# Output and down projections: the left half of the columns over all rows first, beside the side work

## What is computed

```python
def reference(x, ...):
    x = first_block(x, ...)     # mixer (delta rule and HGRN heads), FFN, mixer (NSA attention), FFN
    return second_block(x, ...) # mixer (dilated and MoBA), mixer (differential and stick-breaking), norm
# each mixer: h = rmsnorm(x); proj = h @ w_in; y = heads(proj); y @ w_out is added to x (normed in block 1)
# each FFN:   h = rmsnorm(x); silu(h @ w_gate) * (h @ w_up) @ w_down, normed, added to x
```

## Time and profile before

| what | value |
|---|---|
| time, median of 3 runs | 3078.3 us (3074.62 to 3086.6) |
| time of the profiled execution | 3074.2 us |
| its span, first to last instruction | 3072.4 us |
| TensorE busy | 2878.3 us (94%) |
| VectorE, ScalarE, GpSimd busy | 52%, 46%, 7% |
| mean granted TensorE clock | 0.967 |

### The profile page before, as it was taken

How to read it: one execution, slowest core, us unless ns; L and a number is a source line. 1 busy time by engine, 2 the same in 40 slices (tenths; PEclk the granted TensorE clock), 3 DMA queues, 4 the chain that set the end, 5 groups by cost and what they waited for, 6 DMA issues and landing times.

```text
span 3072.4 us, 33268 instructions
## 1 busy us (share of the span) xinstructions
PE 2878.3 (94%) x13558; PEld 2375.6 (77%) x13558; DVE 1609.7 (52%) x2004; ACT 1401.4 (46%) x2037; POOL 225.2 (7%) x209
## 2 busy tenths in 40 slices
PE   7899999899999999999899989999999999979887
PEld 6788787687888888888777767788888888767665
DVE  5664566646455445445334444655445544555545
ACT  6554444545444444334334444644444433454554
POOL 0112223300000000000100100000000000011011
PEclk9999999999999999999889989999999999988888
DMA  6655443655666666555444424566666655634323
GB/s 201 119 119 129 83 98 83 137 188 175 190 187 190 190 189 189 189 191 194 154 136 136 116 65 155 179 187 192 189 188 189 188 191 190 201 113 137 117 90 109
DMA packets 212777, 480.85 MB, mean 157 GB/s; under 512 B 15249, under 2 KB 16273, under 8 KB 211985
## 3 DMA queue, kind: packets, MB, share of 16 engines
q1 hardware_dynamic: 210272, 467.57, 52.3%
q0 software_dynamic: 2352, 11.17, 1.0%
HBM read 476.58 MB, written 2.10 MB: 156 GB/s over the span
## 4 chain that ended last, share of the span: by engine, by line
PE 80%; DVE 7%; ACT 6%; issue 2%; POOL 2%; DMA 2%; SPq 0%; DVEq 0%; ACTq 0%; POOLq 0%
PE PS L962 17%; PE PS L963 16%; PE PS L964 16%; PE PS L1012 7%; PE PS L1013 7%; PE PS L1011 7%; DVE XL L1948 1%; DVE WL L1948 1%; PE PS L1261 1%; ACT BIG L1531 1%; DVE WORK L2091 1%; PE PS L1341 1%; DVE UTL L1984 1%; PE PS L1122 1%; PE PS L1037 1%
## 5 line engine op out<-in xcount | busy, mean ns | idle before, releaser
L1948 DVE TENSOR_TENSOR WL<-RAW,WH 128x1024 fp32r<-128x1024 f32 x819 | 1016.1, 1241 | 995.1 <-ACT WH L1482 994.3
L1482 ACT ACTIVATE WH<-RAW 128x1024 fp32r<-128x1024 f32 x823 | 867.1, 1055 | 954.4 <-PE PS L964 601.6
L962 PE MATMUL PS<-WH,UTH 128*128 128x512 f32 x2396 | 965.2, 403 | 13.4 <-DVE WL L1948 11.9
L963 PE MATMUL PS<-WL,UTH 128*128 128x512 f32 x2396 | 941.6, 393 | 0.0
L964 PE MATMUL PS<-WH,UTL 128*128 128x512 f32 x2396 | 941.4, 393 | 0.0
L962 PEld LDWEIGHTS PS<-WH,UTH 128*128 128x128 f32 x2396 | 455.9, 190 | 111.8 <-DVE WL L1948 14.3
L964 PEld LDWEIGHTS PS<-WH,UTL 128*128 128x128 f32 x2396 | 454.5, 190 | 98.8
L963 PEld LDWEIGHTS PS<-WL,UTH 128*128 128x128 f32 x2396 | 455.6, 190 | 91.2 <-issue 2.5
L1013 PE MATMUL PS<-WH,HTL 128*128 128x512 f32 x656 | 259.3, 395 | 0.0
L1012 PE MATMUL PS<-WL,HTH 128*128 128x512 f32 x656 | 258.8, 394 | 0.0
L1011 PE MATMUL PS<-WH,HTH 128*128 128x512 f32 x656 | 255.4, 389 | 0.0
(11 more groups left out here) (422 smaller groups left out, 2694.9 us busy)
## 6 DMA issues: line engine op xcount, KB each, us to landing
RAW<-in_ffn_w_gu SPq DMA_DIRECT2D x352, 512.0 KB, 4.1
RAW<-in_ffn_w_down SPq DMA_DIRECT2D x176, 512.0 KB, 4.5
RAW<-in_ab_w_in SPq DMA_DIRECT2D x128, 512.0 KB, 4.7
RAW<-in_nsa_w_in SPq DMA_DIRECT2D x80, 512.0 KB, 3.6
RAW<-in_w_in SPq DMA_DIRECT2D x64, 512.0 KB, 4.1
RAW<-in_ab_w_out SPq DMA_DIRECT2D x32, 512.0 KB, 4.5
RAW<-in_nsa_w_out SPq DMA_DIRECT2D x32, 512.0 KB, 4.5
RAW<-in_w_out SPq DMA_DIRECT2D x16, 512.0 KB, 4.6
```

The source lines that it names most:

```text
L962: e.matmul(o, lh, wh[:, j], start=k + j == 0, stop=False)
L963: e.matmul(o, lh, wl[:, j], start=False, stop=False)
L1482: e.activation(wh, raw, ACTF.Copy).then_inc(*a_hi.inc(s))
L1948: e.tensor_tensor(wl, raw, wh.bitcast(F32), ALU.subtract).then_inc(*v_lo.inc(s))
```

## The change

The rows of every stage run in another order: half 0 over all k-tiles (`left`), then half 1 (`right`); only half 1's last slots are the crossing (eight, in stages 4 and 5 four). `left` belongs to the stage's `main`, so the side generators go on beside it. The operand transposes `ot` become side generators of their own (`operand`): each stands in the list as soon as the last column chunk has read the k-tiles that it overwrites (`read`) and its heads are made. The statistics and products of half 0 move from the crossing into `right`, six and three slots ahead of its last early one. Banks: half 0 takes banks 0 to 3, half 1 banks 4 to 7; the ring of banks for side work stays 4 to 7 beside `left`, where it had all eight at the end of a stage. `stat` of the odd n and `tmp_n` of the even n now free the banks, where `new_h` did.

Around it: `cm_w(0)` is put ahead of stage 2's tables and waits for the end of stage 1's rows; `tables_2` drops its wait for stage 4's first chunk; the extra weight places and the scratch JUNK lie elsewhere; some waits follow the new order.

The core of the diff:

```diff
+TAIL = {0: 8, 1: 8, 2: 8, 3: 8, 4: 4, 5: 4}
+LEFT = {st: range(n) for st, n in KTILES.items()}
+LEFT[0] = (*range(8, 12), *range(4), *range(12, 16), *range(4, 8))
+
+
 def row_order(st):
 
-    n = KTILES[st]
-    order = [(k, hf) for k in range(n) for hf in range(2)]
-    if st in (1, 3):
-        order[0:4] = [(0, 0), (1, 0), (0, 1), (1, 1)]
-    order[-TAIL:] = [(k, hf) for hf in range(2) for k in range(n - TAIL // 2, n)]
-    return order
+
+    return [(k, 0) for k in LEFT[st]] + [(k, 1) for k in range(KTILES[st])]
...
         for _ in main:
             for g in sides:
                 next(g, None)
-        put("pool", range(8))
         while sides:
             sides = [g for g in sides if next(g, "end") != "end"]
...
                     put("col", st, c, k, o.next_slot(), (0, 1))
+                    if c == len(WIDTHS[st]) - 1:
+                        o.done.add(("read", st, k))
...
-        def both(name, t, part):
-            for n in (1, 0) if part == 0 else (3, 2):
-                put(name, st, t, n)
-
-        for j in range(TAIL):
+        for j in range(n_tail):
             o.prep(min(s[j] + 3, c[0]))
             row(j, 0)
-            if j == 3:
-                put("stat", st, 0, 0)
-                both("tmp_n", 0, 0)
-        both("tmp_n", 0, 1)
-        put("stat", st, 0, 1)
+            if st >= 4 and j < 2:
+                halves(st, j, 0)
+        halves(st, 0, 1)
         if st == 5:
             put("fin_s", 0)
-            for j in range(TAIL):
+            for j in range(n_tail):
                 row(j, 1)
-                if j == 3:
-                    both("tmp_n", 1, 0)
-                    put("fin_y", 0)
-            both("tmp_n", 1, 1)
+            put("fin_y", 0)
+            halves(st, 1, 1)
             put("fin_s", 1)
...
-        put("pool", (1, 2, 3))
-        for j in range(TAIL):
+        put("pool", (2, 3, 4, 5))
+        for j in range(n_tail):
             row(j, 1)
             if j < 2:
                 put("new_h", st, 0, 2 * j)
                 put("new_h", st, 0, 2 * j + 1)
                 o.prep(c[j + 1])
-            if j > 3:
-                put("uth", st + 1, j - 4, 0)
-            if j == 5:
-                put("stat", st, 1, 0)
-                both("tmp_n", 1, 0)
+            if j > n_tail - 5:
+                put("uth", st + 1, j - n_tail + 4, 0)
             if 3 < j < 7:
                 o.prep(c[j - 1])
-        both("tmp_n", 1, 1)
...
-        put("stat", st, 1, 1)
+        halves(st, 1, 1)
         put("pool", (4, 5, 6, 7))
         o.slot += 8
         for j in range(8):
+            if n_tail == 4 and j < 3:
+                o.prep(c[j + 3])
...
-    def rows(st):
-        for k, hf in row_order(st)[:-TAIL]:
+    def halves(st, t, part):
+
+        if st < 4:
+            put("stat", st, t, part)
+        for n in (2 * part + 1, 2 * part):
+            put("tmp_n", st, t, n)
+        if st < 4 and part:
+            put("root", st, t)
+
+    def left(st):
+        for k in LEFT[st]:
+            if st not in (1, 3):
+                yield from need(("ot", st, k - k % 2))
+            put("row", st, k, 0, o.next_slot(), (0, 1))
+            yield
+
+    def right(st):
+        put("warm", "rows", st)
+        early = row_order(st)[KTILES[st]:-TAIL[st]]
+        for i, (k, hf) in enumerate(early):
             put("row", st, k, hf, o.next_slot(), (0, 1))
-            yield
-
-    def out_proj(st):
-        for k in range(0, KTILES[st], 2):
-            put("ot", st, k)
-        put("warm", "rows", st)
-        drain(rows(st))
-        cross(st)
+            if i in (len(early) - 6, len(early) - 3):
+                halves(st, int(i == len(early) - 3), 0)
+
+    def operand(st, k, *made):
+        yield from need(("read", st, k), *made)
+        put("ot", st, k)
...
             yield from cols(st, sink)
-            put("warm", "rows", st)
-            put("pool", (6, 7))
-            yield from rows(st)
+            yield from left(st)
...
         together(main(), hidden())
+        right(st)
         cross(st)
...
-        put("cm_w", 0)
...
-    together(cols(0, lambda c, t: put("z", EVEN[c][0], t)), convs(), gdn(), hgrn(),
-             out_gate(1, 0), out_gate(0, 0), out_gate(1, 1), out_gate(0, 1))
+    def mixer(st, sink, *sides):
+        def main():
+            yield from cols(st, sink)
+            yield from left(st)
+
+        together(main(), *sides)
+
+    mixer(0, lambda c, t: put("z", EVEN[c][0], t), convs(), gdn(), hgrn(),
+          out_gate(1, 0), out_gate(0, 0), out_gate(1, 1), out_gate(0, 1),
+          *[operand(0, k, ("og_m", k // 8, k % 8 // 4)) for k in LEFT[0] if k % 2 == 0])
     put("gb", 0)
-    out_proj(0)
+    right(0)
+    cross(0)
     ffn(1)
+    put("cm_w", 0)
     put("tables_n")
-    together(cols(2, lambda c, t: put("n", NSA[c][0], t)), compress(), keys(0), keys(1),
-             *[stream(u, i) for u in range(2) for i in range(2)])
+    mixer(2, lambda c, t: put("n", NSA[c][0], t), compress(), keys(0), keys(1),
+          *[stream(u, i) for u in range(2) for i in range(2)],
+          *[operand(2, k, *[("pv", k // 4, i, 2) for i in range(2)]) for k in range(0, 16, 2)])
     put("gb", 2)
-    out_proj(2)
+    right(2)
+    cross(2)
     ffn(3)
     put("tables_2")
     put("gb", 4)
     sink2 = {st: lambda c, t, st=st: put("z2", st, PARTS2[c], t) for st in (4, 5)}
-    together(cols(4, sink2[4]), setup(4, 0, True), setup(4, 2, True),
-             *[plain(br, par, i) for br in range(2) for par in range(2) for i in range(2)],
-             *[close(4, br, 2 * br + 1, *[[("pl_o", br, par, i) for par in range(2)] for i in range(2)])
-               for br in range(2)])
-    out_proj(4)
+    mixer(4, sink2[4], setup(4, 0, True), setup(4, 2, True),
+          *[plain(br, par, i) for br in range(2) for par in range(2) for i in range(2)],
+          *[close(4, br, 2 * br + 1, *[[("pl_o", br, par, i) for par in range(2)] for i in range(2)])
+            for br in range(2)],
+          *[operand(4, k, *[("y2", 4, k // 2, i) for i in range(2)]) for k in (0, 2)])
+    right(4)
+    cross(4)
     put("lam")
-    together(cols(5, sink2[5]), setup(5, 0, True), setup(5, 2, False),
-             *[diff(h, i) for h in range(4) for i in range(2)], *[stick(h) for h in range(4)],
-             close_diff(), close(5, 1, 3, *[[("st_o", h) for h in range(4)]] * 2))
-    out_proj(5)
+    mixer(5, sink2[5], setup(5, 0, True), setup(5, 2, False),
+          *[diff(h, i) for h in range(4) for i in range(2)], *[stick(h) for h in range(4)],
+          close_diff(), close(5, 1, 3, *[[("st_o", h) for h in range(4)]] * 2),
+          operand(5, 0, ("y2d", 0), ("y2d", 1)), operand(5, 2, ("y2", 5, 1, 0), ("y2", 5, 1, 1)))
+    right(5)
+    cross(5)
...
+        last_ot = {a[1]: a[2] for a in ORDER if a[0] == "ot"}
         col_end = {(a[1], a[2]): a[4] for a in ORDER if a[0] in ("col", "nar")}
 
         home, before, held = [], [], [None] * (NW + NX)
         for s in range(len(slots)):
-            extra = any(v[-1] - TAIL + 2 < s <= v[-1] or v[-1] + 3 < s <= v[-1] + 8 for v in row_slots.values())
+            extra = any(v[-1] - TAIL[st] + 2 < s <= v[-1] or v[-1] + 3 < s <= v[-1] + 8 for st, v in row_slots.items())
...
+            return p_mm.of(row_slots[st][KTILES[st] + 33]) if st in (1, 3) else p_ut.of("ot", st, last_ot[st])
 
         def row_end(st, t, part):
 
-            s = row_slots[st][-1] - (TAIL // 2 if part == 0 else 0)
+            if part == 0:
+                return p_mm.of(row_slots[st][KTILES[st] - 1])
+            s = row_slots[st][-1]
...
+        def row_bank(st, t, n):
+
+            return 4 + 2 * t + n - 2 if n > 1 else 2 * (t ^ len(WIDTHS[st]) % 2) + n
...
-                if k == 0:
+                if k == (0 if hf else LEFT[st][0]):
                     for t in ts:
                         for n in range(2):
-                            banks.take([4 * t + 2 * hf + n], "row", st, t, 2 * hf + n)
+                            banks.take([row_bank(st, t, 2 * hf + n)], "row", st, t, 2 * hf + n)
                             on.wait_ge(*banks.free("row", st, t, 2 * hf + n))
...
-                for n in (0, 1) if part == 0 else (2, 3):
+                for n in (2 * part, 2 * part + 1):
                     on.wait_ge(*a_nm.last())
                     if n % 2:
                         on.wait_ge(*v_nm.of("tmp", st, t, n))
+                    up = banks.empty(a_nm, "row", st, t, n) if n % 2 else a_nm.inc("ms", st, t, n)
                     e.activation(JUNK, banks.ap("row", st, t, n), ACTF.Square,
-                                 accum_out=MSQ[:, 4 * t + n:4 * t + n + 1]).then_inc(*a_nm.inc("ms", st, t, n))
-                if part:
-                    rstd(1, "post", st, t)
+                                 accum_out=MSQ[:, 4 * t + n:4 * t + n + 1]).then_inc(*up)
+
+            @step
+            def root(st, t):
+                rstd(1, "post", st, t)
...
+                if st in (1, 3):
```

(10 more changed lines are left out.)

39 lines of the change are left out of this document (16 added, 23 removed).

## The result

The changed kernel takes 3045.65 us (median of 4, 3034.09 to 3047.31) beside 3078.13 (3074.62 to 3086.6) of the kernel before in the same runs: a ratio of 0.9882, 95% interval 0.9851 to 0.9914. Its profiled execution took 3045.93 us with a span of 3044.1. The forecast was 3046 and -30; the spans differ by 28.3.

The account below looks back on a forecast made before the run. It took TensorE's instruction stream, plus 194 us idle and low-clock time, as the bound; terms summed to -29.8, say -30, from 3074.2 to 3044.2, and half the distance to the median gave 3046, range 3020 to 3066.

Parts of the forecast that it names:

- crossings of stages 0 to 3: Crossings of stages 0 to 3: TensorE's pauses behind split weights nearly go, -15 us (bounds 0 and 17.5 gained).
- end of stage 2: After stage 2's last column slot: side work runs beside left rows instead of alone, -11 us (bounds -4 and -19).
- end of stage 0: Stage 0, last column to first row: left rows run beside the last gate, with a 5.6 wait; -5 us (-12 to +2).
- left banks in stages 1 and 3: Stages 1 and 3, left half: first row waits 1.5 us each for the last up chunk's banks, +3 (0 to 3.5).
- tables_2: Stage 4's tables: loads no longer wait for the first chunk, so the rotation ends earlier, -7.4 us.
- cm_w(0): Load issued a crossing earlier: TensorE's 2.4 us wait at L1261 goes, -2.4 (bounds -2.4 and +3).
- stage 4: Stage 4: rows' stretch 5.4 us shorter, against a 4.6 operand wait in the last column chunk and 2 of low clock; +1.
- stage 5: Stage 5: rows gain 4 us, but operand 0 waits 11.2 for both y2d in the columns; +7 (0 to +15).
- the row 1690 to 1800 (0.98): Stretch of side work beside columns with short pauses, clock 0.98; taken to show that interleaved left halves would not run slow.
- far from 1: Sign of being wrong: granted clock in the left halves of stages 0 and 2 far from 1; no size given.
- (a): Rival: the operand waits in stages 0, 4 and 5 are not there, 25 us fall away, 3021; chance 12%.
- (c): Rival: low clock beside interleaved rows in the mixer stages' left halves; half of them slow costs +54, 3102; chance 6%.

Follow-up runs that it names:

- late_all: The changed kernel with all operand transposes that TensorE waits for put later, in stages 4 and 5 k = 0 behind the last column chunk; 3022.0 us, ratio 0.9814.
- late_mid: As late_all, but stages 4 and 5's operand transposes of k = 0 stand inside the last column chunk, two to four slots behind their producer; 3015.9 us, ratio 0.9809.

## Why the prediction was right, term by term

| term | forecast | measured | by |
|---|---|---|---|
| crossings of stages 0 to 3 | -15 | -16.1 | of the 17.5 of pauses behind XL only 0.74 and 0.71 are left, in stages 1 and 3 |
| end of stage 2 | -11 | -9.3 | rows 149.9 to 138.7, less the crossing's 1.9 |
| end of stage 0 | -5 | -5.2 | columns + rows 697.4 to 690.4, less 1.9 |
| left banks in stages 1 and 3 | +3 | +3.2 | L1040 behind L2047, 1.59 twice |
| `tables_2` | -7.4 | -6.7 | wait ahead of `feat` 12.8 to 6.2 |
| `cm_w(0)` | -2.4 | -1.1 | waits of L1261 2.4 + 2.2, now 3.5 |
| stage 4 | +1 | +0.4 | rows -5.8; columns -3.0, without the -2.5 and -6.7 that stand above +6.2 |
| stage 5 | +7 | +7.2 | columns +9.2, rows -4.0, tail +2.0 |
| sum | -29.8 | -28.3 | spans |

The measured terms add up to -27.6; the -0.7 left over lies within what the same stretches differ by from kernel to kernel. The total is closer than its terms, as misses of both signs cancel (the crossings gave 1.1 us more than forecast, stage 2, `cm_w(0)` and `tables_2` together 3.7 less). And that 3046 met 3045.65 is luck: the changed kernel's own executions lie between 3034.1 and 3047.3.

*Crossings.* Mechanism and size are shown: each half put back brings its own pause back. The 0.3 us a pass that the forecast left to the DMA ring are 0.7 in two passes and under 0.2 in the others.

*End of stage 0.* The chain read from the planner's order was right to 0.1 us: the wait behind the last gate was forecast at 5.6 and is 5.5. late_all shows that it was the place in the order and not the chain: eight slots later it is gone, and stage 0's rows are 2.1 us shorter beyond it. The sum of -5.2 is known less well than that, because stage 0's columns, which are in it, spread by some 4 us.

*Stage 5.* The forecast wait was 11.2, the measured one 9.3: `y2d` was done some 2 us earlier relative to the columns. GpSimd in order of time, as in the earlier trace rows, where its last product took 1.60:

```profile
2977.98 0.72 POOL L2640 TENSOR_TENSOR BIG<-BIG 128x256 f32<-128x256 f32 x1 [2.44 <-DVE BIG L2429]
2978.78 0.72 POOL L2643 TENSOR_TENSOR BIG<-BIG,WORK 128x256 f32<-128x256 f32 x1
```

The last products take 0.72 each; VectorE has no weight to split while TensorE stands, and the last section takes this up. The low clock after the wait was put at 2.5 us; behind it the 19.1 us of matmuls run at 0.88, 2.3 us:

```profile
2979.60:2998.76 19.16, 19.11 (x76) 15.48 (x76) 8.05 (x7) 6.85 (x7) 0.00 (x0) 0.88 0.43 136
```

That +7 met +7.2 is again a balance: the columns grew by 9.2 where 10.7 were forecast, and rows and tail together shrank by 2.0 where 4 were. The last tile's result waits 2.0 us behind the first's on VectorE, not 1.1, and the rows have a wait of 3.24 behind `y2` where 2.4 were counted.

*End of stage 2.* The pauses were right: 5.2 + 2.5 + 1.8 + 1.1 + 0.5 = 11.1 us in this stretch for the 11.6 counted. The longest of them stands behind `pv`, where the forecast had 3:

```profile
1866.90 1.07 PE L1057 MATMUL PS<-MK,BIG 128*128 128x128 f32 x8 [2.21 <-POOL BIG L2595]
```

What was too small is the low clock. The forecast's 32 us of busy time left 4.1 for it over the 27.9 at full clock, and the prediction argued from the row 1690 to 1800 (0.98) that interleaved work runs near full clock; the left half ran at 0.90, and 0.10 x 70.7 = 7 us went there. In stage 0 the left half (605.57 to 658.65) ran at 0.94. The prediction had named "far from 1" as a sign of being wrong without a number for it; 0.90 is between its 0.98 and the 0.75 of the lone side work. This is the place where the Trainium skill (TensorE: Matmul & The Clock Gate, "A second HAM failure mode: psum-queue depth-cycling"), by which short pauses between groups of matmuls can make the clock swing, spoke against the change. The trace agrees in part: with the pauses the clock is a tenth down, and the stretch is still 9.3 us shorter than lone side work at 0.75.

*Stage 4.* The wait for `y2` was put at 4.6 and is 3.7. With waits of 2.9 for `pl_t` (L1410, which the list before hasn't got) that makes 6.6 us for the +6.2 in the columns; these 2.9 the forecast didn't see, and the 2 us of low clock that it counted aren't needed. The near match (+0.4 for +1) is made of both.

*`cm_w(0)`.* The step that failed is "takes away the 2.4": behind the load stood VectorE's block copies, 1.3 us later. What was late next wasn't asked.

*`tables_2`.* Forecast to 5.4, measured 6.2, behind VectorE's rotation rather than GpSimd's: 0.7 us.

Two of the rivals were nearer to the matter than their chances. (a), operand waits not there, is a kernel that can be had by placing the transposes: late_mid is this kernel, 3016 (by its ratio 0.9809 x 3078.3 = 3019) where (a) said 3021. And (c), low clock from waits, has its place after all: in the left half of stage 2 it took 7 us, far from the 54 of (c), and in stage 2's columns it took 15.6 us in the changed kernel's profile. It was there in the kernel before as well (columns of 347.9), and the prediction walked past it.

## What to carry to other kernels

Where several engines work off one written order, ask of every step of the bounding engine how far behind its producer it stands: too near costs a wait, and putting it behind the next stage's work costs another (here 9.3 and 7.3 us for the same operand, 0 in between). The cover is a slot or more of the main stream put between, as long as the chain's end keeps its place in the order. A wait can cost more than its length, as low clock can add to it: 8.2 us of waits went with 24 in stage 2's columns, while a pause of 1.9 put back into the crossings of stages 1 and 3 cost 1.4 and 1.6. So waits of 1 to 3 us among side work deserve more attention than their sum. And compare kernels stage by stage before comparing times: twice here a stage that the edit didn't touch hid the edit.
